# Moving two matmul operand buffers to other byte offsets in SBUF

## The reference

```python
proj = h @ w_in                       # (256, 1024) @ (1024, columns)
x = x + dsa_mixer(...)                # projections, attention, projection
x = x + conv_ffn(...)                 # u = h @ w_up ; (silu(a) * b) @ w_down
x = x + retention_mixer(...)
x = x + conv_ffn(...)
x = x + gate_m * hybrid_mixer(...)    # SSD and pooling, both projected
x = x + gate_f * (square(relu(h @ w_up)) @ w_down)
```

## Time and profile before

| | us |
|---|---|
| median of three executions | 1196.7 |
| the profiled execution | 1195.99 |
| its span, first to last instruction | 1194.2 |
| granted TensorE clock, share of full speed | 0.997 |

### The profile page before, as it was taken

One profiled execution on the slowest core, in us unless ns is written; L12 is line 12 of the kernel. 1 busy time (PEld: TensorE's weight loads), 2 busy tenths in 40 slices (PEclk: granted clock), 3 DMA queues, 4 the chain that ended last, 5 costly groups with the idle time before them and its releaser, 6 DMA issues.

```text
span 1194.2 us, 25488 instructions
## 1 busy us (share of the span) xinstructions
PE 1171.9 (98%) x9034; PEld 1117.0 (94%) x9034; DVE 975.3 (82%) x1774; ACT 713.0 (60%) x1111; POOL 33.3 (3%) x62
## 2 busy tenths in 40 slices
PE   9999999999999999999999999999999999999997
PEld 7988999999899999999999989999999899999996
DVE  7867998887998888889888789999996677666666
ACT  6576665555455456556565577877866456544553
POOL 0000000000000110000000000000000000000000
PEclk9999999999999999999999999999999999999999
DMA  7534676664566866856655437458545556655550
GB/s 277 189 97 168 201 234 233 220 225 164 189 249 235 296 247 230 275 186 239 219 203 190 155 125 249 138 190 184 184 155 200 181 189 211 197 191 181 189 176 36
DMA packets 72752, 235.71 MB, mean 197 GB/s; under 512 B 7392, under 2 KB 16096, under 8 KB 72560
## 3 DMA queue, kind: packets, MB, share of 16 engines
q1 hardware_dynamic: 64016, 203.86, 51.3%
q0 software_dynamic: 8528, 30.98, 7.4%
q10 hardware_dynamic: 144, 0.02, 0.0%
HBM read 233.73 MB, written 1.09 MB: 197 GB/s over the span
## 4 chain that ended last, share of the span: by engine, by line
PE 86%; DVE 7%; issue 3%; ACT 3%; DMA 1%; DVEq 0%; SPq 0%; ACTq 0%
PE ps L199 26%; PE ps L200 25%; PE ps L201 25%; PE ps L231 3%; DVE w_lo L191 2%; PE ps L232 2%; ACT w_hi L186 1%; DVE arena L1912 1%; PE ps L1579 1%; DMA w_raw<-stream 1%; DMA arena<-x 0%; DVE arena L1900 0%; DVE arena L451 0%; PE ps L1221 0%; ACT L331 0%
## 5 line engine op out<-in xcount | busy, mean ns | idle before, releaser
L199 PE MATMUL ps<-a_hi,w_hi 128*128 128x256 f32 x1656 | 468.5, 283 | 4.1 <-DVE w_lo L191 2.0
L191 DVE TENSOR_TENSOR w_lo<-w_raw,w_hi 128x1024 fp32r<-128x1024 f32 x381 | 460.7, 1218 | 10.3 <-ACT w_hi L186 4.5
L200 PE MATMUL ps<-a_lo,w_hi 128*128 128x256 f32 x1656 | 463.4, 280 | 0.0
L201 PE MATMUL ps<-a_hi,w_lo 128*128 128x256 f32 x1656 | 462.8, 279 | 0.0
L186 ACT ACTIVATE w_hi<-w_raw 128x1024 fp32r<-128x1024 f32 x381 | 390.5, 1048 | 24.4 <-PE ps L201 16.3
L199 PEld LDWEIGHTS ps<-a_hi,w_hi 128*128 128x128 f32 x1656 | 311.8, 188 | 9.7 <-issue 5.0
L200 PEld LDWEIGHTS ps<-a_lo,w_hi 128*128 128x128 f32 x1656 | 311.6, 188 | 0.5
L201 PEld LDWEIGHTS ps<-a_hi,w_lo 128*128 128x128 f32 x1656 | 311.0, 188 | 0.0
L199 PE MATMUL ps<-b_both,w_hi 128*128 128x256 f32 x560 | 157.3, 281 | 4.8 <-DVE b_both L920 4.2
L200 PE MATMUL ps<-b_both,w_hi 128*128 128x256 f32 x560 | 156.6, 280 | 0.0
L201 PE MATMUL ps<-b_both,w_lo 128*128 128x256 f32 x560 | 156.3, 279 | 0.0
(11 more groups left out here) (305 smaller groups left out, 1665.9 us busy)
## 6 DMA issues: line engine op xcount, KB each, us to landing
w_raw<-stream SPq DMA_DIRECT2D x381, 512.0 KB, 4.0
arena<-ada POOLq DMA_DIRECT2D x48, 512.0 KB, 5.5
c_both<-cum_rows POOLq DMA_DIRECT2D x4, 1024.0 KB, 7.7
arena<-x SPq DMA_DIRECT2D x2, 512.0 KB, 4.3
con<-consts SPq DMA_DIRECT2D x1, 1024.0 KB, 5.9
arena<-row_cols POOLq DMA_DIRECT2D x2, 512.0 KB, 4.5
out<-arena SPq DMA_DIRECT2D x4, 256.0 KB, 2.2
arena<-c_rows POOLq DMA_DIRECT2D x1, 512.0 KB, 4.1
```

The lines of the kernel that those rows point to most:

```text
L191: dve.tensor_tensor(w_lo[:, s % RING], w_raw[:, s % RING], w_hi[:, s % RING].bitcast(F32), ALU.subtract).then_inc(w_lo_ready, 1)
L199: pe.matmul(o, wh, xh, start=start, stop=False, skip_group_check=shared)
L200: pe.matmul(o, wh, xl, start=False, stop=False, skip_group_check=shared)
L201: return pe.matmul(o, wl, xh, start=False, stop=stop, skip_group_check=shared)
```

## The change

The spacer ahead of `a_hi` becomes 8 float32 = 32 bytes, and a second spacer of 16 float32 = 64 bytes goes in between `a_lo` and `b_both`. `a_hi` and `a_lo` then start 32 bytes off a multiple of 128 and `b_both` 96 bytes off; before, it was 64 for both. The offset of the weight rings stays 0. Everything behind `b_both` moves up by 32 bytes: `c_both` tile k starts at 96 + 16k. In `keep_going` the list has two entries with twelve matmuls each in place of six with four; with `b_both` at 96 their offsets are (112, 96) and (16, 96).

```diff
-        sb("between", [P, LINE])
+        sb("between", [P, 8])
         a_hi, a_lo = sb("a_hi", [P, NT, SEQ], F32R), sb("a_lo", [P, NT, SEQ], F32R)
+        sb("between_too", [P, 16])
         b_both = sb("b_both", [P, 2 * NT, 2, SEQ], F32R)
...
         idle_operand = b_both[:, 0:4].rearrange("p m i t -> p (m i t)")
-        IDLE = ((4, 4), (16, 16), (1, 1), (8, 0), (0, 32), (128, 0))
+        IDLE = ((4, 0), (12, 0))
...
                 for moving, still in IDLE:
-                    for _ in range(4):
+                    for _ in range(12):
                         pe.matmul(ps[:, 5, 0:SEQ], idle_operand[:, still:still + P], idle_operand[:, SEQ * 4 + moving:SEQ * 5 + moving], start=True, stop=True)
```

## The result

The changed kernel takes 1197.93 us, median of 20 executions (1195.09 to 1200.18). In the same comparison the kernel before takes 1195.64 us (20 executions, 1192.64 to 1198.08). The ratio is 1.002, 95% interval 1.0012 to 1.0028: slower by 0.2%, where 0.5% faster was forecast. The profiled execution took 1198.89 us, 2.9 us more than the one of before, and its span, too, is 2.9 us longer.

A forecast was written before the change was run, and what follows sets the result against it. TensorE's matmul stream was taken to bound the kernel, number of matmuls times distance between starts. The `a` term of -6.0 us, all others 0, took 1195.99 to 1189.99, plus 0.7 for the median: 1190.7 us, range 1173 to 1207.

The forecast's parts named there:

- What bounds the kernel: Whole kernel: a TensorE stream at full granted clock; the change acts only through the distance between matmul starts.
- The ruler: Matmul stream: a matmul's duration tells its pace; 4 ns of duration stand for 4.7 ns of distance between starts.
- `a` from 64 to 32: 4968 matmuls moving `a_hi`/`a_lo` against weights at 0: 1.2 ns less distance each, 6.0 us less.
- `b_both` as moving operand: 2016 matmuls moving `b_both`, from 64 to 96: 0, bounds 9.5 us less to 4.8 us more.
- slower, if it hits `b`: Stationary load and moving stream collide more often at 96: 4.8 us more, 1201.5 us; all slower cases together 0.32.
- `b_both` as stationary operand: 576 matmuls with `b_both` or `a_hi`/`a_lo` pieces stationary, 512 columns moved: 0, with 3.5 us less or more.
- `c_both`: About 1000 matmuls in the groups of `c_both`, tiles from 64 + 16k to 96 + 16k: 0, with 2 us each side.
- The list: The 24 unused matmuls, hidden behind a TensorE wait: 0, or 0.1 us if that cover went.
- The pages: Two skill rules, 16-byte cachelines and two independent read ports, speak against any effect: no term, 1196.7 us.
- The short pace: Stream at `a`, `b_both` or both locks on 4.7 ns less distance per matmul: 1164 to 1187 us, chance 0.17.

The follow-up runs named there:

- e2: Kernel before with only `b_both` moved from 64 to 96 and all behind it by 32; 1199.84 us, ratio 1.0066.
- e7: Kernel before, unused matmuls replaced by probe stretches with stationary operand at 64, then 512-column stretches at eight stationary offsets; 1282.54 us with its added matmuls.
- e4: Kernel before, unused matmuls replaced by 16 stretches of 48 at eight moving offsets, each twice, stationary operand at 0; 1284.13 us with 744 matmuls more.
- e12: Kernel before, unused matmuls replaced by 28 pairs: 12 at one moving offset, then 36 at another, stationary at 0; 1348.03 us with 1320 matmuls more.
- e6: The change's two offsets exchanged, `a` at 96 and `b_both` at 32; 1206.91 us, ratio 1.0098 to the kernel before.
- e17: Same edit as e1 (only `a` to 32, `b_both` at 64), measured again in another session; 1192.44 us, ratio 0.9977 to the kernel before.
- e3: Kernel before with only the list of unused matmuls changed, both buffers at 64; 1190.86 us, ratio 0.9996.
- e1: Kernel before with only `a_hi` and `a_lo` moved from 64 to 32, `b_both` staying at 64; 1192.92 us, ratio 1.0007.
- e13: Kernel before, both buffers at 64, plus 12 unused matmuls reading `a_hi` at 16 in each feed-forward; 1194.53 us, ratio 0.9984.
- e16: As e13 with 4 unused matmuls in place of 12; 1196.42 us, ratio 0.9985 to the kernel before.

## Why the prediction was wrong

**What bounds the kernel** was right: the counts are the same, and the offsets act through the distance between starts, 2.2 us of it. It took the full granted clock for given, though. Stretches of 3.4 us at half of it come in both kernels, from none to two ahead of the last microseconds in the profiles here, and one cost 1.5 us, more than half of what the offsets cost.

**The ruler** (duration for distance) was right. 282 ns for `b_both` gives 118.0 + 2.4 = 120.4, and 120.0 was measured in e2; 279 gives 116.8, and `a` in the second feed-forward has 116.65.

**`a` from 64 to 32, forecast -6.0 us: sign right, size wrong.** The pace brought 1.9 us. The sample it rested on, four matmuls at (96, 64), stands for a difference of 32, and e7 and e4 have 116.6 and 116.7 for a difference of 32 by long stretches. The second feed-forward and later stages show it. The first feed-forward doesn't: `a` at 32 has 117.96 there. There is more than one pace at 32, as in e12 after 0. Part of the rest is that some stages of before were quick already: `a` had 113.3 in the stage of the earlier trace rows and has 116.7 there now.

**`b_both` as moving operand, forecast 0: the step that failed.** It cost 1776 x 1.85 = 3.3 us, more than `a` gave, and made the sign. By size the term of `a` was missed by more, 4.1 us. With either term alone as forecast, the sum would still have come out 1 to 2 us faster; it took both to turn it. The step read the pace at 96 from single tiles of `c_both`, 258 columns wide, each with neighbours at other offsets. There the offset moves on with every tile, so no row showed a steady stream at 96. It also compared the tile at 96 with the tile at 64, 282 ns both, and not with the 280 ns of `b_both` itself; by the prediction's own ruler 282 is 120.4 ns. Steady streams at 96 have 120.0, 119.8 and 119.9 ns in e4, e2 and e6. The rival "slower, if it hits `b`" had priced it at 4.8 us and was the case that came, together with the small gain of `a`; the prediction didn't cross the two. Against an execution that enters 64 from 32, as in e17, 96 costs more: 1776 x 4.3 = 7.6 us (119.64 less 115.34).

**`b_both` as stationary operand, forecast 0 with 3.5 us to each side:** +0.4 us, and e7 has the same 1.1 ns in a stretch of its own. **`c_both`, 0 with 2 us:** +0.4 us; e2, with `c_both` at the same place, has the same 120.40 ns. **The list, 0:** right, by e3.

**The pages.** All offsets of e4 are multiples of 16 bytes, and its paces reach from 113.3 to 120.0 ns. By the rule of the Trainium skill ("SBUF — State Buffer", "Specifications (TRN2)") on 16-byte cachelines they would cross equally many lines; the trace doesn't agree that this is all. Moving 64 gives 117.8 ns with the stationary operand at 0 and 120.0 with it at 64 (e4, e7). The two independent read ports that the Trainium skill has ("TensorE: Matmul & The Clock Gate", "Step-by-step: what each phase is for") would leave no such dependence; the trace doesn't agree with that either, for float32r. Why the difference matters was not measured.

**The chances.** The short pace was given 0.17, as a result of the new offsets. In the kernel it was seen at 64 alone, which the change gives up. The earlier trace rows had shown it, and the prediction asked only whether a new offset would find it, not how often the old one does.

**Open:** why 112 holds 113.3 in a probe and 118.7 in the kernel; what picks the pace at a stall or an entry, since the offset before it doesn't settle it (e1, e4, e13); what starts a stretch at half clock; and the lower times of e13 and of three executions of e16, which no profile caught.

## What to carry to other kernels

In a stream of float32r matmuls bound by TensorE, the byte offset of the moving operand against the stationary one, modulo 128, is worth up to 6% of the distance between starts. Measure it in stretches of 48 in the pattern of the kernel, and then in the kernel, since 112 didn't carry over here and 32 only in some stages. The best kernel tried had `a` at 32 and `b_both` at 64, and 96 was slow for whichever buffer lay there. Before trusting a change of 0.3%, see in more than one profile which pace the kernel before runs in, and how long each execution stood at half clock.

## What the runs showed that was not expected

- The distance between starts of 256-column matmuls keeps coming back to a few values: 113.3, 116.7, 117.8, 118.3, 118.7 and 120.0 ns, all in stretches at the full granted clock. At half the granted clock it is 213 ns.
- At one offset there can be two of them, steady over hundreds of matmuls (1342 in e3) and taken at an entry. In e12, 64 after 16, 32 or 48 has 113.3, after 0, 80, 96 or 112 it has 117.8; in e4 after 48 and in e13 after 16 it has 117.8 instead.
- With a difference of 0 to 48 bytes only the difference counts, not the two offsets (e4, e7). With 512 columns it is otherwise: stationary 0 and 16 have 227 ns, 32 to 112 have 232 to 234.
- The same program differs between executions by up to 10 us (1187.42 to 1197.63), and the profiles differ where its stages fall into one pace or the other; one feed-forward is worth 6.1 us. The granted clock is a second part: in the comparison of e13 the median of before is 1195.0 us where the clock of the whole span was 0.998 (4 executions) and 1198.0 where it was 0.995 (6).
